# The first block's modulation rows: summed in column tiles of TensorE during the attentions and kept, in place of products on VectorE

## The chip, the cores and the metric

One core of one Trainium2 chip runs the whole program. The metric is the device time of one execution in microseconds. The kernel is written by hand for each engine's queue: PE (TensorE), ACT (ScalarE), DVE (VectorE), POOL (GpSimd) and SP (SyncE, which issues most weight loads). Everything is fp32.

## The reference

Two blocks of two layers each run on 256 latent tokens of width 1024 (two tiles of 128, called tiles 0 and 1). The second block also carries 256 context tokens (tiles 2 and 3).

```python
# first block, for l in 0, 1
mod = silu(c) @ w_ada[l] + b_ada[l]          # [1024] x [1024, 6144]
sh_m, sc_m, gt_m, sh_f, sc_f, gt_f = split(mod, 6)
h = rms_norm(x, g_pre_mix[l]) * (1 + sc_m) + sh_m
y = token_mixer(h, w_in[l], ..., w_out[l])   # two attentions, 8 heads each
x = x + gt_m * rms_norm(y, g_post_mix[l])
h = rms_norm(x, g_pre_ffn[l]) * (1 + sc_f) + sh_f
y = conv_glu_ffn(h, w_up_act[l], w_up_lin[l], ..., w_down[l])
x = x + gt_f * rms_norm(y, g_post_ffn[l])
# second block: an even layer (attention and short conv), then PEER experts,
# an odd layer (mLSTM), then PEER experts; rows for latents and for context
mod_l = split(silu(c_2) @ w_mod[i] + b_mod[i], 6); mod_c = the same with c_ctx_2
```

A modulation vector (6 of 1024 numbers a layer, 12 halves of 512) is one row, a product of one vector with a 25 MB matrix. What the kernel needs is the row spread over all 128 partitions, times a gain where there is one.

## The kernel before

**Streams and order.** The context's even layer, queries and first experts (`context`) don't depend on the first block, so each engine's program merges the two: `merged(first(lane, l), beside)` takes a step of the first block and then as many steps of the context stream as the shares (CH, ATT, PACE) ask for. All five queues are written in the same merged order, and every engine runs its queue in order. Four steps of the context stream (`AHEAD`) come before the first block begins. A background stream (`lane.run(mods, name)`) is taken a step at a time by `lane.fill(n, name)` and to its end by `lane.flush(name)`.

**Stages of the first block, each layer.** `lin` w_in (29 chunks of up to 512 KB), index scores, attention in ten steps of ATT 1.2 (layer 0) or 0.5 (layer 1), w_out in 8 chunks, feed-forward up in 44 chunks, down in 22. The context's queries (16 units, peer_w_q in two chunks every second unit) stand beside the attention of layer 0, and its 256 experts (each an indirect gather of 1 MB by POOL, a dot product on DVE L2244 and a weighted sum on PE L2186 or DVE L2239) beside all that follows.

**Modulation rows, three ways.** `Mods`: SP fetches pieces [128, 512] of the weight (256 KB), DVE multiplies each by a column of silu(c) and adds it to an accumulator (the first piece in L369, seven in L371), and PE sums over the partitions with a matmul of ones and adds the bias (L406, L408), which gives the row on all partitions; DVE (L381, L384) or ACT (L393) writes it into its place in MOD. `PairMods` (the context rows of layer 0 of the second block): no products; eight matmuls whose stationary operand is 32 columns wide, into four column groups of a bank by turns (L492), a bias matmul (L497), a copy on ACT (L516), a small DMA that keeps four rows in BR, and a matmul that adds and spreads the groups (L504). `KeptMods`: one matmul spreads a row kept in BR (L595). The first block uses `Mods` for all its halves, under these keys:

- ada0a (layer 0, shift and scale, 4 halves), at the start, after the four context steps, from 16 slots of 512 KB that were fetched early (`WIDE_L`);
- ada0b (layer 0, the other 8 halves), a quarter of a half behind each w_in chunk of layer 0, in 7 buffers of 256 KB;
- ada1a (layer 1, 6 halves), the same behind each feed-forward up chunk of layer 0;
- ada1b (layer 1, 6 halves), the same behind each w_in chunk of layer 1.

`keep1` and `keep2` are `Mods` too (w_mod of layer 1 of the second block, kept for later, 16 accumulators) and run in the context's even layer. The context's own rows come in `PairMods`: mod0c1 first of all, then mod0c2, a half behind each context step from the first on, through the four chunk buffers of RAW.

Of the kernel before, what the change touches and what calls it, by code (L numbers as in the profile page):

```python
# [118 lines left out]
def program(nc, D, out):  # L119
    with ExitStack() as ctx:  # L120
# [41 lines left out]
        def view(buf, a, *dims):  # L162
# [14 lines left out]
        AF = [T[:, 512 * i:512 * i + 512] for i in range(2)]  # L177
        OWN_T = [T[:, a:a + 512] for a in (1536, 3072, 3584)] + [HTt[:, 2048 + 512 * i:2560 + 512 * i] for i in range(4)]
        OWN_BIG = [BIG[:, 5632 + 512 * i:6144 + 512 * i] for i in range(3)] + [T[:, 1024 + 512 * i:1536 + 512 * i] for i in range(4)]
        ACS = [BIG[:, 512 * i:512 * i + 512] for i in range(2)]  # L180
# [5 lines left out]
        WIDE_L = [BIG[:, 1024 * i:1024 * i + 1024] for i in range(1, 7)] + [HTt[:, 1024 * i:1024 * i + 1024] for i in range(4)] + [  # L186
            T[:, 1024:2048]] + [SL[:, 1024 * i:1024 * i + 1024] for i in (3, 4, 8, 9, 10)]
        AHEAD = 4
# [84 lines left out]
        class Mods:  # L273

            def __init__(self, key, w, row0, jobs, accs, frees, guard=(), every=1, own=(), wide=()):
                self.own, self.named, self.wide = own, "own", wide
                self.ring = SIDE if not wide else FIRST[0] if accs else EARLY
# [155 lines left out]
        class PairMods(Mods):  # L434
# [3 lines left out]
            def __init__(self, key, w, row0, jobs, frees, guard=(), wide=()):  # L438
                Mods.__init__(self, key, w, row0, [(j, [(2, dst, kind, gain)]) for j, dst, kind, gain in jobs], None,
                              frees, guard, wide=wide)  # L440
                self.count = len(self.halves) + 1

# [39 lines left out]
            def sums(self, pe, q):  # L482
                j, hh, outs = self.halves[q]
                bk = bank(pe, self.ring, "pair", self.key, j, hh)
                pe.wait_ge(("silu",))
                for kh in range(4):
                    pe.wait_ge(("raw", self.key, j, hh, kh))
                    wt = self.pair_of(j, hh, kh)
                    for c in range(2):
# [3 lines left out]
                                            CP[:, 32 * kc:32 * kc + 32], wt[:, c, :],  # L493
# [16 lines left out]
            def copied(self, a, q):  # L510
                j, hh, outs = self.halves[q]
                a.wait_ge(a.last, ("mm", "pair", self.key, j, hh))
                if q >= 2:
                    a.wait_ge(("kept", *self.halves[q - 2][:2]), ("mm", "mod", self.key, *self.halves[q - 2][:2], 0))
                a.wait_ge(self.guard)
# [3 lines left out]
            def keep(self, a, q):  # L519
                j, hh, outs = self.halves[q]  # L520
                r = 48 + 4 * (2 * j + hh)
                a.wait_ge(("ev", "pair", self.key, j, hh))
                a.eng.dma_start(BR[r:r + 4, :], self.row(q)[0:128:32, :]).then_inc(*land.landed(f"kept{2 * j + hh}", "kept", j, hh))
# [5 lines left out]
            def dve(self, v):  # L529
                return self.each(v, lambda *_: None, self.out_dve)  # L530

# [28 lines left out]
        class KeptMods(Mods):  # L560
# [43 lines left out]
            def dve(self, v):  # L604
                return self.each(v, lambda *_: None, self.out_dve)

# [274 lines left out]
        def start_sp(sp):  # L881
# [4 lines left out]
            next(rows)  # L886
            sp.eng.dma_start(Xt[:, 2:4, :], D["ctx_2"].rearrange("(t p) d -> p t d", p=128)).then_inc(
# [3 lines left out]
        def second_rows_sp(sp):  # L891
            through(mods_of["start"].steps(sp))
# [2114 lines left out]
```

## Time and profile before

| | us |
|---|---|
| median of 3 runs | 3621.55 (3619.16 to 3630.48) |
| the profiled execution | 3621.2 |
| its span | 3619.9 |
| PE, DVE, ACT, POOL busy | 2892.3, 2313.7, 1136.4, 981.6 |
| DVE L371, products of the modulation rows, x280 | 212.7 |
| PE L492, PE L1114 | column tiles of the context rows; feed-forward up |

The page counts the fp32 matmuls in two records each, so x8 is four matmuls. Times in the rows are microseconds from the span's start unless ns is said.

### The profile page before, as it was taken

Reading aid. Unit: us, or ns where it says so; the run is one execution under the profiler, and the core shown is the slowest. Engines: PE = TensorE matmul, PEld = TensorE weight load, DVE = VectorE, ACT = ScalarE, POOL = GpSimd, SP = SyncE. Lnnn points to the kernel's source line nnn. Section 1 sums busy time; section 2 is a strip of 40 time slices with the busy share of each in tenths; the row PEclk is TensorE's granted clock in tenths of the full one; section 3 lists DMA queues with packets and bytes.
Section 4 is the critical chain, followed back from the end, with each engine's and each line's share of the span. In section 5 each row is a group of like instructions: output and inputs, shape, how many; then the busy total and the mean of one; then the engine's idle time right before and its main releaser. Section 6 shows DMA issues by size and latency. Waiting matters only on the chain.

```text
span 3619.9 us, 30466 instructions
## 1 busy us (share of the span) xinstructions
PE 2892.3 (80%) x9297; PEld 1538.4 (42%) x9297; DVE 2313.7 (64%) x4862; ACT 1136.4 (31%) x2905; POOL 981.6 (27%) x841
## 2 busy tenths in 40 slices
PE   5688967679988768987778777798779788777776
PEld 1344446356533336834446333343354463332222
DVE  0556538789867667875764998544423459975544
ACT  1112122323322352313451444333323224443333
POOL 0000000222332223332321444444310015443332
PEclk8789978689999889998879999899998889999999
DMA  8555732689979758997864999899962259999997
GB/s 333 173 191 204 248 123 94 227 343 363 358 288 409 273 205 323 417 408 262 315 242 157 392 421 421 347 420 421 421 238 75 70 211 419 421 421 421 422 421 332
DMA packets 214564, 1108.80 MB, mean 306 GB/s; under 512 B 24948, under 2 KB 25408, under 8 KB 116096
## 3 DMA queue, kind: packets, MB, share of 16 engines
q0 software_dynamic: 114512, 818.87, 56.1%
q1 hardware_dynamic: 99040, 287.27, 21.9%
q8 instruction: 73, 1.20, 0.1%
q10 hardware_dynamic: 848, 0.72, 0.1%
q14 instruction: 91, 0.75, 0.1%
HBM read 1105.58 MB, written 1.05 MB: 306 GB/s over the span
## 4 chain that ended last, share of the span: by engine, by line
PE 31%; DMA 29%; DVE 28%; ACT 4%; issue 4%; SPq 1%; POOL 1%; ACTq 0%; DVEq 0%; POOLq 0%
DMA AR<-in_uv,AR 24%; PE PS L805 9%; DVE AR L2244 7%; PE PS L2175 5%; PE PS L2088 3%; DMA AR<-in_w_in 2%; DVE AR L371 2%; PE PS L1127 2%; PE PS L1602 2%; DVE AR L2239 2%; PE PS L2186 2%; PE PS L787 1%; PE PS L2326 1%; DMA AR<-in_even_w_in 1%; DVE AR L1975 1%
## 5 line engine op out<-in xcount | busy, mean ns | idle before, releaser
L2294 POOL DMA_INDIRECT AR<-in_uv,AR x768 | 909.2, 1184 | 1577.9 <-PE PS L2175 641.3
L2244 DVE CUSTOM_DVE_ANT_0 AR<-AR 128x1024 f32<-128x1024 f32 x768 | 937.1, 1222 | 505.3 <-DMA AR<-in_uv,AR 503.2
L2175 PE MATMUL PS<-AR 128*128 128x512 f32 x2048 | 971.0, 622 | 288.6 <-ACT AR L2231 282.7
L2175 PEld LDWEIGHTS PS<-AR 128*128 128x128 f32 x2048 | 386.0, 196 | 867.1 <-ACT AR L2231 453.4
L805 PE MATMUL PS<-AR 128*128 128x512 f32 (+3 forms) x1080 | 470.5, 587 | 46.2 <-DMA AR<-in_w_in 20.8
L2213 ACT ACTIVATE AR<-AR 128x2 f32<-128x2 f32 x384 | 78.1, 203 | 1143.3 <-DVE AR L2244 1142.2
L1114 PE MATMUL PS<-AR 128*128 128x256 f32 x1408 | 322.1, 388 | 15.8 <-DMA AR<-in_w_up_lin 11.6
L805 PEld LDWEIGHTS PS<-AR 128*128 128x128 f32 x1080 | 204.1, 203 | 292.7 <-issue 241.7
L1114 PEld LDWEIGHTS PS<-AR 128*128 128x128 f32 x1408 | 269.9, 194 | 79.3 <-issue 19.7
L371 DVE SCALAR_TENSOR_TENSOR AR<-AR,CC 128x512 f32<-128x512 f32 x280 | 212.7, 760 | 67.5 <-DMA AR<-in_w_ada 44.6
L2231 ACT ACTIVATE AR<-C,AR 128x128 f32<-128x128 f32 (+1 forms) x614 | 241.0, 392 | 20.2
L2227 ACT ACTIVATE AR<-AR 128x1 f32<-128x1 f32 x768 | 226.1, 294 | 25.1
L2239 DVE SCALAR_TENSOR_TENSOR AR<-AR 128x1024 f32<-128x1024 f32 x152 | 196.4, 1292 | 9.2 <-ACT AR L2227 4.0
L2088 PE MATMUL PS<-AR 128*128 128x256 f32 x768 | 184.3, 402 | 4.0 <-DVE AR L641 3.2
L861 ACT ACTIVATE AR<-PS 128x256 f32<-128x256 f32 (+5 forms) x250 | 110.9, 443 | 234.5 <-PE PS L2088 113.3
L2213 ACT ACT_TABLE_LOAD x81 | 103.9, 1283 | 249.4 <-DVE AR L2244 249.3
L1127 PE MATMUL PS<-AR 128*128 128x512 f32 x352 | 161.6, 613 | 19.1 <-DVE AR L1357 8.3
L2186 PE MATMUL PS<-AR 64*64 64x512 f32 x816 | 126.8, 704 | 55.5 <-ACT AR L2231 53.8
L2088 PEld LDWEIGHTS PS<-AR 128*128 128x128 f32 x768 | 154.2, 204 | 28.0 <-issue 2.8
L1534 POOL TENSOR_TENSOR X<-X,AR 128x512 f32<-128x512 f32 x12 | 15.2, 1264 | 533.9 <-DVE AR L1526 533.9
L624 PE MATMUL PS<-C,AR 128*128 128x128 f32 x254 | 56.2, 393 | 117.4 <-DVE AR L714 47.8
L1127 PEld LDWEIGHTS PS<-AR 128*128 128x128 f32 x352 | 66.6, 195 | 113.6 <-issue 82.7
(235 smaller groups left out, 2652.4 us busy)
## 6 DMA issues: line engine op xcount, KB each, us to landing
AR<-in_w_ada SPq DMA_DIRECT2D x160, 256.0 KB, 8.1
AR<-in_w_in SPq DMA_DIRECT2D x56, 512.0 KB
AR<-in_w_mod SPq DMA_DIRECT2D x96, 256.0 KB, 4.5
AR<-in_peer_w_q SPq DMA_DIRECT2D x48, 512.0 KB
AR<-in_w_mod SPq DMA_DIRECT2D x45, 512.0 KB, 12.6
AR<-in_w_up_act SPq DMA_DIRECT2D x44, 512.0 KB
AR<-in_w_up_lin SPq DMA_DIRECT2D x44, 512.0 KB
AR<-in_w_down SPq DMA_DIRECT2D x44, 512.0 KB
```

The lines of the kernel that those rows point to most:

```text
L371: v.eng.scalar_tensor_tensor(out=acc, in0=wt, scalar=col, in1=acc, op0=ALU.mult, op1=ALU.add).then_inc(*v.done(*end))
L805: ins = pe.eng.matmul(bk[:, 0:n], lhs(k0 + kc, t), wt[:, kc, :], start=(k0 + kc == 0), stop=(k0 + kc == nk - 1))
L1114: ins = pe.eng.matmul(bk[:, f * 256:f * 256 + 256], wt[:, kc, cs], LAT.all[:, k0 + kc, :], start=(k0 + kc == 0 and f == 0), stop=(k0 + kc ...
L1127: ins = pe.eng.matmul(bs[t, hh], GT[:, f, t * 128:(t + 1) * 128], wt[:, 0, hh * 512:(hh + 1) * 512], start=(f == 0), stop=(f == 21))
L2088: ins = pe.eng.matmul(bk[:, f * 256:f * 256 + 256], wt[:, kc, cs], e.lay.all[:, k0 + kc, :], start=(k0 + kc == 0 and f == 0), stop=(k0 + k ...
L2175: ins = pe.eng.matmul(acc[i][hh], e.dg(x), e.buf(x)[:, 1024 + 512 * hh:1536 + 512 * hh], start=(x == e.on[False][i][0]), stop=(x == e.on[F ...
L2186: ins = pe.eng.matmul(acc[r][cols, :], e.dg(x)[rows, :], e.buf(x)[rows, 1024 + 512 * c:1536 + 512 * c], start=(x == e.on[False][x // 128][ ...
L2227: a.eng.activation(w, w, ACT.Copy, scale=gw_at(x // 16, x % 16, 1)).then_inc(*a.done(*(("w", e.key, x) if e.on_dve(x) else ())))
L2231: a.eng.activation(e.dg(x), cst("id2") if e.halved else ident, ACT.Copy, scale=w).then_inc(*a.done("dg", e.key, x))
L2239: v.eng.scalar_tensor_tensor(out=ACC, in0=row, scalar=w, in1=ACC, op0=ALU.mult, op1=ALU.add).then_inc(*v.done("sum", e.key, x))
L2244: v.eng.tensor_tensor_reduce(e.buf(x)[:, 0:1024], e.buf(x)[:, 0:1024], norm2(e).H[e.tiles[x // 128]], 1.0, 0.0, ALU.mult, ALU.add, DT[x // ...
L2294: g.eng.indirect_dma_start(e.buf(x), None, D["uv"][e.l], bass.IndirectOffsetOnAxis(ap=idx_at(x // 16, x % 16, 1), axis=0)).then_inc(*land. ...
```

## The change

The pieces of w_ada are no longer multiplied on DVE.

- **Start.** ada0a becomes `OneMods`, a `PairMods` with its own 32-wide columns `CP1` and without the DMA that keeps rows. Its steps run on every engine right behind mod0c1, ahead of the four context steps; those carry no mod0c2 half any more, since mod0c2 begins only after the fourth. The small conv rows are issued by POOL and no longer by SP; the context's norm is scaled early.
- **Layer 0, attention.** A stream "q", `Quads` "early", makes 12 halves: 8 of layer 0 and the 4 of layer 1's shift and scale. A step fetches four pieces [128, 512], one of each of four halves, and sums them with four matmuls of a 32-wide stationary operand, each half in its own column group of one bank. Eight steps and the biases make four halves; ACT copies the bank, and one DMA keeps four rows in BR (rows 112 to 127). There are five piece buffers (`OWN_Q`), in places of MOD and T, and SP waits for the score of the index (`("sco", 0, 1)`) before the first. One step stands before the attention, one behind each attention step, and one behind each of the context's query steps.
- **Layer 1, attention.** `Quads` "later" makes the other 8 halves of layer 1 the same way, with one step before, two behind each of the first five attention steps and one behind the others (`QUICK`).
- **Rows to their places.** `KeptAda` spreads a kept row with one matmul and lets DVE or ACT write it, as `KeptMods` does: 8 halves in each w_out (`fill(2)` a chunk), 4 halves in the feed-forward of layer 0. Nothing runs behind the w_in chunks.

```diff
+        OWN_Q = [MODt[:, 2048 + 512 * i:2560 + 512 * i] for i in range(3)] + [T[:, 3072 + 512 * i:3584 + 512 * i] for i in range(2)]
+        ROWS_Q = MODt[:, 3584:4096]
...
             def each(self, lane, made, put):
                 for q in range(len(self.halves)):
-                    if q:
+                    if q and not self.wide:
                         put(lane, q - 1)
                     made(lane, q)
+                    if q and self.wide:
+                        put(lane, q - 1)
                     yield
...
+        class Quads:
...
+            def sp(self, sp):
+                n = len(OWN_Q)
+                for q, (r0, halves) in enumerate(self.quads):
+                    for kc in range(8):
+                        for g, (l, r) in enumerate(halves):
+                            i = self.piece(q, kc, g)
+                            sp.wait_ge(("quad", self.key, i - n) if i >= n else self.guard)
+                            sp.eng.dma_start(OWN_Q[i % n], D["w_ada"][l][r, kc // 2, :, 512 * (kc % 2):512 * (kc % 2) + 512]).then_inc(
+                                *land.landed(f"quad{i % n}", "raw", self.key, i))
+                        yield
+                yield
+
+            def pe(self, pe):
+                n = len(OWN_Q)
+                for q, (r0, halves) in enumerate(self.quads):
+                    bk = bank(pe, SIDE, "quad", self.key, q)
+                    pe.wait_ge(("silu",))
+                    for kc in range(8):
+                        for g, (l, r) in enumerate(halves):
+                            i = self.piece(q, kc, g)
+                            pe.wait_ge(("raw", self.key, i))
+                            pe.eng.matmul(bk[32 * g:32 * g + 32, :], CC[:, kc:kc + 1].to_broadcast([128, 32]), OWN_Q[i % n],
+                                          start=(kc == 0), stop=False).then_inc(*pe.done("quad", self.key, i))
...
+                        yield
+                yield
+
+            def keep(self, a, q):
+                r0, halves = self.quads[q]
+                a.wait_ge(a.last, ("mm", "quad", self.key, q), ("kept", self.key, q - 1) if q else self.free)
+                a.eng.activation(ROWS_Q, psum("quad", self.key, q), ACT.Copy).then_inc(*a.done("ev", "quad", self.key, q))
+                a.wait_ge(a.last)
+                a.eng.dma_start(BR[r0:r0 + 4, :], ROWS_Q[0:128:32, :]).then_inc(*land.landed("keptq", "kept", self.key, q))
...
+        class KeptAda(KeptMods):
...
+            def spread_out(self, pe, q):
+                j, hh, outs = self.halves[q]
+                r = self.rows[j] + hh
+                bk = bank(pe, self.ring, "mod", self.key, j, hh, 0)
+                pe.wait_ge(self.made)
+                pe.eng.matmul(bk, ident[96:128, r:r + 1].to_broadcast([32, 128]), BR[96:128, :], start=True,
+                              stop=True).then_inc(*pe.done("mm", "mod", self.key, j, hh, 0))
...
+        def attended(lane, l, steps):
+
+            for i, _ in enumerate(steps):
+                lane.fill(1 + (i < QUICK[l]), "q")
+                yield ATT[l]
...
         def first_pe(pe, l):
             n1, n2 = norm_of["f", l, 1], norm_of["f", l, 2]
-            pe.run(mods_of["first", l])
-            for i, _ in enumerate(lin_pe(pe, ("win", l), D["w_in"][l], 8, (0, 3656), [0, 1], LAT.tile, prep=n1, ring=FIRST[l],
-                            whole=HEAD[l])):
-                if i >= 4 * len(HEAD[l]):
-                    pe.fill()
-                yield CH
-            pe.flush()
+            for _ in lin_pe(pe, ("win", l), D["w_in"][l], 8, (0, 3656), [0, 1], LAT.tile, prep=n1, ring=FIRST[l], whole=HEAD[l]):
+                yield CH
...
+            pe.flush("c")
+            pe.run(mods_of["quads", l], "q")
+            pe.fill(1, "q")
             yield 1.0
...
-            for _ in stages(8, s1, s2, s3):
-                yield ATT[l]
+            yield from attended(pe, l, stages(8, s1, s2, s3))
+            pe.flush("q")
+            pe.run(mods_of["first", l])
             yield 1.0
...
-                yield CH
+                pe.fill(2)
+                yield CH
+            pe.flush()
             pe.run(mods_of["next", l])
...
         def context(lane, even, queries, experts):
 
-            lane.run(cmods, "c")
             lane.run(Ready(keep1, keep2), "keep")
             for i, share in enumerate(even(lane, "c")):
+                if i == AHEAD - 1:
+                    lane.run(cmods, "c")
                 lane.fill(1 if i >= AHEAD else 0, "keep")
                 yield PACE * share
             lane.flush("keep")
             lane.run(cgate, "c")
             for share in queries(lane, of_ctx):
+                lane.fill(1, "q")
                 yield PACE * share
```

The other engines' programs of the first block are changed as `first_pe` is.

## Rows read from the trace of the kernel before

**Rows 1.** The page: chain by engine; GB/s in 40 slices.
```profile
PE 31%; DMA 29%; DVE 28%; ACT 4%; issue 4%; SPq 1%; POOL 1%; ACTq 0%; DVEq 0%; POOLq 0%
...
GB/s 333 173 191 204 248 123 94 227 343 363 358 288 409 273 205 323 417 408 262 315 242 157 392 421 421 347 420 421 421 238 75 70 211 419 421 421 421 422 421 332
```

**Rows 2.** Stretches: length, busy PE, PEld, DVE, ACT, POOL, clock, DMA share, GB/s.
```profile
0.00:50.00 50.00, 25.37 (x96) 7.28 (x96) 7.45 (x13) 10.86 (x19) 4.35 (x8) 0.81 0.98 377
134.00:460.00 326.00, 281.49 (x843) 145.45 (x842) 182.35 (x319) 50.16 (x119) 6.36 (x7) 0.92 0.67 228
541.00:627.00 86.00, 69.85 (x362) 59.92 (x361) 71.59 (x240) 24.28 (x84) 2.67 (x5) 0.86 0.27 89
740.00:960.00 220.00, 196.66 (x896) 143.61 (x895) 205.79 (x422) 74.19 (x151) 62.80 (x46) 0.97 0.98 379
1080.00:1240.00 160.00, 134.72 (x454) 57.85 (x452) 118.55 (x221) 38.23 (x95) 39.78 (x30) 0.95 0.92 365
1240.00:1345.00 105.00, 67.01 (x360) 39.66 (x360) 76.53 (x165) 51.75 (x139) 22.54 (x20) 0.76 0.53 187
```

**Rows 3.** Timeline of the start: us, duration, engine, line, operation.
```profile
46.24 0.36 SPq L253 DMA_DIRECT2D AR<-in_even_w_in  x1
...
59.39 5.88 PE L805 MATMUL PS<-AR 128*128 128x416 f32 x8 [14.60 <-DMA AR<-in_even_w_in]
...
93.67 0.49 DVE L369 TENSOR_SCALAR AR<-AR,CC 128x512 f32<-128x512 f32 x1
...
134.53 4.75 PE L805 MATMUL PS<-AR 128*128 128x512 f32 x8
```

**Rows 4.** Chain that ended last, in order of time, context steps.
```profile
76.86 3.03 DMA AR<-in_even_w_in
...
79.93 3.06 PE PS L805 x8
82.99 0.87 PE PS L504 x2
...
84.54 1.09 PE PS L492 x8
85.63 3.25 DMA AR<-in_even_w_in
```

**Rows 5.** Chain by line, 134 to 541 us.
```profile
by line: PE PS L805 30.7%; PE PS L1602 10.5%; PE PS L408 6.5%; DVE AR L371 5.8%; PE PS L406 5.7%; PE PS L2088 4.2%; DMA AR<-in_w_in 3.8%; DMA AR<-in_even_w_in 3.1%; issue 2.2%; PE PS L653 2.0%; DMA AR<-in_w_mod 1.8%; PE PS L492 1.7%; DVE AR
```

**Rows 6.** Line 302, SyncE's issues of 256 KB pieces: ns min/median/max, and landings.
```profile
L302 SPq DMA_DIRECT2D AR<-in_w_ada x160: 327/432/2986, 135.6 to 1191.6; - x160
...
DMA to landing us min/median/max: 2.5/5.0/23.7
```

**Rows 7.** Timeline, attention of layer 0: w_q chunk pairs (first, last of six), scores.
```profile
530.99 0.71 PE L2099 MATMUL PS<-AR 128*128 128x128 f32 x4
...
536.72 8.58 PE L2088 MATMUL PS<-AR 128*128 128x256 f32 x32 [0.87 <-ACT AR L861]
...
540.52 0.42 DVE L1414 TENSOR_TENSOR AR<-AR,C 128x256 f32<-128x256 f32 x1
...
616.57 7.13 PE L2088 MATMUL PS<-AR 128*128 128x256 f32 x32
```

**Rows 8.** Timeline, layer 1: the index scores are ready.
```profile
1245.30 0.42 DVE L1414 TENSOR_TENSOR AR<-AR,C 128x256 f32<-128x256 f32 x1
```

**Rows 9.** The page's DMA issues: a gain's broadcast.
```profile
MOD<-in_g_post_mix POOLq DMA_DIRECT2D x2, 512.0 KB, 7.0
```

**Rows 10.** DMA in 740 to 960 us, then in 1080 to 1240.
```profile
DMA packets 20157, 83.42 MB, mean 379 GB/s; under 512 B 2241, under 2 KB 2241, under 8 KB 14653
...
AR<-in_w_ada SPq DMA_DIRECT2D x46, 256.0 KB, 8.5
...
DMA packets 15320, 58.37 MB, mean 365 GB/s; under 512 B 1708, under 2 KB 1708, under 8 KB 11604
...
AR<-in_w_ada SPq DMA_DIRECT2D x44, 256.0 KB, 14.5
```

More of the change, by code:

```diff
@@ L886, in start_sp @@
             next(rows)
+            next(rows)
             sp.eng.dma_start(Xt[:, 2:4, :], D["ctx_2"].rearrange("(t p) d -> p t d", p=128)).then_inc(
@@ L916, in start_act, with second_rows_act @@
             first_rows(a)
+        def second_rows_act(a):
+            rows = mods_of["start"].steps(a)
+            next(rows)
+            next(rows)
+            next(rows)
+            norm_of["f", 0, 1].squares(a, ("pair", "ada0a", *mods_of["start"].halves[0][:2], 0))
+            through(rows)
         def start_dve(v):
@@ L1176, in first_pool @@
             n1, n2 = norm_of["f", l, 1], norm_of["f", l, 2]
[L1177 to L1180 removed]
+            for _ in lin(g, 8, (0, 3656), [0, 1], nothing, prep=n1):
                 yield CH
[L1182 removed]
             yield 1.0
@@ L1187, in first_pool @@
                     *land.landed(f"go{i}", "go", l, i))
+            g.flush("c")
+            g.run(mods_of["quads", l], "q")
+            g.fill(1, "q")
             yield 1.0
-            for _ in range(10):
-                yield ATT[l]
+            yield from attended(g, l, range(10))
+            g.flush("q")
+            g.run(mods_of["first", l])
             yield 1.0
             for _ in lin(g, 8, (0, 1024), [0, 1], nothing):
+                g.fill(2)
                 yield CH
+            g.flush()
             add_pool(g, l, 2, ("mix", l))
@@ L1298, in s2 @@
                                  ("mm", "av", l, u - 2) if u >= 2 else None).then_inc(*a.done("ev", "pt", l, u, kt))
-            for _ in stages(8, s1, s2, nothing):
-                yield ATT[l]
+            yield from attended(a, l, stages(8, s1, s2, nothing))
+            a.flush("q")
+            a.run(mods_of["first", l])
             for t in range(2):
@@ L1477, in s3 @@
                 v.events["ev", "av", l, u] = v.last
-            for _ in stages(8, s1, s2, s3):
-                yield ATT[l]
+            yield from attended(v, l, stages(8, s1, s2, s3))
+            v.flush("q")
+            v.run(mods_of["first", l])
             rs = []
@@ L1494, in first_dve @@
             for _ in lin(v, 8, (0, 1024), [0, 1], nothing):
+                v.fill(2)
                 yield CH
-            add_dve(v, l, 2, ("lin", "wout", l), mods_of["first", 0] if l == 0 else mods_of["next", 0])
+            v.flush()
+            add_dve(v, l, 2, ("lin", "wout", l), mods_of["first", l])
             v.run(mods_of["next", l])
```

208 lines of the change are left out of this document (128 added, 80 removed).

## The prediction

> **What bounds the kernel now.** I read the page first. No engine is full over the span, and the chain that ended last is shared by PE, DMA and VectorE [rows 1]: a change is worth what it does to the stage it lies in, so everything below goes by stage. The changed work all lies in the front, before 1400 us; behind it the slices are at 420 GB/s of gathered experts, which the change doesn't touch, so what the front gains or loses should come out at the end.
>
> The table by stretches [rows 2] cuts the front at its stages. To 134 us (the start) the first 50 us are a full DMA, then it falls away. From 134 to 460 PE is busy over 80% (projections of both streams). From 541 to 627, and again from 1240 to 1345, lie the attentions of the first block: DMA moves only 89 and 187 GB/s. From 740 to 960 (feed-forward of layer 0) and from 1080 to 1240 (projection of layer 1) DMA runs at 379 and 365 GB/s, and in the first VectorE is busy 206 of 220 us as well.
>
> **The start.** The timeline [rows 3] and the chain [rows 4] show it. SyncE issues w_ada, x and small conv rows up to 46.2 us, and only then the first even_w_in chunk, which PE uses at 59.4. Each of the four context steps that follow takes 8.8 us (76.86 to 85.63), of which 3.06 are its matmuls; the rest is one half of the context rows. At 93 VectorE begins the 32 products of ada0a, some 26 us of work, and PE begins w_in only at 134.5. After the change the conv rows leave SyncE's queue, the four steps carry no half, and the four halves of ada0a are summed on PE as they land. By bytes: 377 GB/s over 50 us [rows 2] is 18.9 MB, just the 16.8 MB of these weights and the two inputs, so all are in at about 50, the last row made about 3.5 us later, 56 at most. Four context chunks and two turns on PE are some 18 us (53 to 72), then conv rows 1.3, norm and turn of the latents about 7: w_in starts at 80 instead of 134.5. **-54** (bounds -45, -60).
>
> **134 to 541.** Three context halves were made here; now all seven steps of that stream are. A step costs 5.7 us beyond its chunk where nothing else runs [rows 4], and also uses up the four chunk buffers; I take 7 each, +28 for four (bounds 15, 35). Gone are the 8 halves of ada0b. The chain's shares of VectorE's products (L371) and of the two matmuls a half (L406, L408) are 5.8, 5.7 and 6.5%, 18% of these 407 us [rows 5], 73 us for 24 accumulators (8 of ada0b, 16 of the keeping streams). A third is 24; with VectorE and SyncE also less in the way of the others I take 30 (bounds 24, 45). Together **-2**.
>
> **The attentions.** This is where the change pays. 96 pieces of 256 KB, 24 steps of four, go into the attention of layer 0, and 64 in 16 steps into that of layer 1. In layer 0 a step is put behind each attention step and behind each query step of the context, about three to an attention step, so they are through after some seven; nothing is left to flush. Column tiles four at a time: before, eight records (four matmuls) take 1.09 us, one full 512-column matmul 0.87 [rows 4], so I take 1.1 us of PE for a step. The price is the wait. There are five buffers, and SyncE may issue piece i only when PE has used i-5; its issue takes 0.43 us, and a piece of these queues needs 2.5 us at the least and 5.0 in the middle [rows 6]. The third of a step's four issues is what the next step needs: 3 times 0.43 plus 2.5 to 5.0 is 3.8 to 6.3, so a step can't follow the last in under about 5 us. SyncE's queue has the w_q chunks behind these waits, one step ahead only. In layer 0 two w_q chunks come each 16 us (536.72 to 616.57, five gaps) [rows 7], of which 7 us are the chunk's matmuls; with it 7+1, then two steps at 5, one of them covered by attention's own work, is 18: +2.1 us, 7.5 times, +16. Besides, the first piece waits for the scores, ready at 540.9 [rows 7], while PE stands at its first step since some 531 and has the score matmuls of unit 0 and w_q behind it; with some 4.5 us to land and a second step before unit 0, VectorE gets it at some 552 instead of 541: +11. Layer 0: **+27** (bounds 10, 55). In layer 1 five attention steps of 8 us carry two steps each: 5 of PE's own work, 1, then 5 of waiting is 11, five times +3; six single ones at +1; the scores are ready at 1245.7 [rows 8], +6. That is **+27** (bounds 12, 55).
>
> The Trainium skill, in DMA: Bandwidth & Descriptors, section Anatomy of one DMA, puts a transfer at 2.0 us plus its bytes by 436 GB/s; the estimate for a step by it (2.0 us and four pieces) is 4.4 us, and the sum would be some 14 us lower. The loaded landings of [rows 6] are slower than it, so I stay at 5. Its TensorEngine Tiling (Array Packing), section Key Properties, speaks against the change: switching the tiling mode drains the engine, and here 40 steps switch it to and fro. The 1.09 us of [rows 4] came right behind full-width work, so a drain of 0.2 us, 8 us over 40 steps, is already in my 1.1; a larger one no row shows.
>
> **The output projections.** Eight halves of kept rows are spread in each (0.87 us of PE, +7), and now right where the gains arrive: POOL issues each gain with its half, a broadcast takes 7.0 us to land [rows 9], VectorE waits for it, and PE's next half waits for the one bank. Three gains, some 4 us beyond a chunk's 3.6 each, would be 12; gathers are waited for there anyhow, so I take 5. **+12** in each layer (bounds 7, 20).
>
> **Feed-forward of layer 0.** Out go 46 of ada1a's 48 pieces that were issued here, 12 of 83.42 MB [rows 10]: 71.4 MB at 379 GB/s are 188 us against 220. VectorE loses 42 products and 6 first ones, 34.5 of 205.8 us, to 171; PE loses 12 matmuls, 12.9 us, and gets 4, 3.5 us, 187 left of 196.7 [rows 2, 10]. DMA and PE meet at 188: **-30** (bounds -18, -34).
>
> **Projection of layer 1.** 44 pieces, 11.5 of 58.37 MB, which at about 400 GB/s are 29 us; nearly all the stretch is at that rate, and PE's 134.7 us go to 123 [rows 2, 10]. With the pieces just ahead of it, **-30** (bounds -20, -34).
>
> **Sum.** -54 -2 +27 +12 -30 -30 +27 +12 = -38. The profiled execution took 3621.2 us (span 3619.9); the median of the runs is 3621.55, so the two are one. I predict **3583 us**.
>
> **Rivals.** (1) Slower: the five-piece ring is the new bottleneck of both attentions. A step costs two waits a round in layer 0 (15 us of span for each us of the step's time) and about 7 us for each us in layer 1. From 5 to 8 us (w_ada pieces took 8.5 where DMA was full [rows 10]) that is +66: 3649. It decides from about 6.7 us a step on. For it: in-order PE, and SyncE behind the same waits; against: DMA has room there. (2) No change: the freed bytes of the two full stretches come to nothing, because PE, already busy 197 of 220 and 135 of 160 us, sets them. Then they give 10 each, and the sum is +2: 3623. (3) The start's gain goes back, the seven context steps now standing in a stretch where PE is 85% busy with 8.8 us each and the relief of VectorE there off the path: +7 and +15 on the second term, 3605. (4) Better: waits in the attentions are covered by VectorE, busy 72 of 86 us there [rows 2], and cost half, 27 in all for both; the projections 7 each: 3546.
>
> **How the numbers follow.** A measurement of this kernel tells 0.3%, 11 us, from nothing. My forecast, with (3) as its weaker form, 0.52; (4) 0.15; (2) 0.12; (1) 0.21. Faster is the forecast's and (4)'s 0.67, same 0.13, slower 0.20. The forecast's own range is 3555 to 3608; for 8 in 10 it reaches toward (1) and past (4): 3532 to 3636.
>
> **What would show it.** First w_in matmul near 80 us; in both attentions PE waiting for in_w_ada, steps 5 us apart, the stretches 541 to 627 and 1240 to 1345 each some 27 us longer; no L371 on w_ada, 112 left for keeping; the feed-forward stretch at some 190 us with VectorE under 90%; the projection of layer 1 at 130. The prediction is wrong if a step in the attentions takes over 6.7 us, if w_in starts later than 95, or if the feed-forward stays above 205.

## The result and the profile after

| | before | after |
|---|---|---|
| median of 20 runs each | 3622.41 (3612.43 to 3632.04) | 3638.92 (3626.26 to 3649.85) |
| ratio | | 1.0042, interval 1.0033 to 1.0052 |
| profiled execution | 3621.2, span 3619.9 | 3629.07, span 3627.8 |

The changed kernel is 0.42% slower, 16.5 us by the medians. The forecast was 3583 us, faster, with a range to 3636: the sign was wrong, and the median lies 3 us above the range. The profiled execution is one of the faster ones, so its trace shows 8 of the 16.5 us; the runs spread over 24 us, and where the other 8 lie no trace here shows.

The page after, its chain by engine, which answers to [rows 1], and two rows of its groups:

```profile
PE 41%; DMA 29%; DVE 19%; ACT 5%; issue 3%; POOL 2%; SPq 1%; ACTq 0%; DVEq 0%; POOLq 0%
...
L665 PE MATMUL PS<-MOD,CC 128*32 128x512 f32 x194 | 83.7, 693 | 59.6 <-DMA MOD<-in_w_ada 50.0
L370 DVE SCALAR_TENSOR_TENSOR AR<-AR,CC 128x512 f32<-128x512 f32 x112 | 86.4, 772 | 44.5 <-DMA AR<-in_w_mod 40.6
```

The products are gone from VectorE as foreseen (112 of 280 left, 28% of the chain down to 19), but PE's share went from 31 to 41%. The windows of the attention of layer 0, the feed-forward up of layer 0, the attention and the w_out zone of layer 1, which answer to [rows 2] (same columns):

```profile
472.00:648.00 176.00, 142.70 (x644) 74.22 (x645) 91.76 (x300) 32.42 (x109) 8.62 (x11) 0.91 0.68 235
752.00:938.00 186.00, 182.27 (x881) 137.47 (x881) 170.89 (x378) 74.21 (x151) 62.89 (x45) 1.00 0.97 371
1187.00:1291.00 104.00, 74.13 (x416) 28.87 (x416) 54.39 (x131) 40.83 (x111) 13.14 (x14) 0.83 0.82 278
1291.00:1392.00 101.00, 64.01 (x200) 25.89 (x196) 41.02 (x61) 25.25 (x62) 20.53 (x17) 0.79 0.55 195
```

The feed-forward stretch is 186 us at 371 GB/s, VectorE 170.9 busy, as forecast. The attention of layer 0 is 176 us, with VectorE busy only 92 of them.

The next table cuts both traces, and those of four experiments below, at the same places: first 512-column w_in matmul, second score of the index ready (VectorE), last value matmul of the attention, first up matmul, last down matmul, and so on for layer 1. The place "last value matmul" is the start of the value matmuls of the last two of the eight units in layer 0 and of the last unit in layer 1. Each entry is a stretch's length less that of the kernel before, in us, from the starts of matmuls and instructions in the traces (before: 134.5, 406.0, 106.1, 92.3, 304.0, 202.4, 65.2, 71.8, 247.1).

```
                    forecast  after  a_start  d_ring9  g_all  m_late_T
start                  -54    -50.1   -50.3    -50.4   -50.0   -50.5
to scores, layer 0      -2    -18.8   +29.5    -19.1   -19.0   -17.5
attention 0            +27    +69.9    +0.1    +31.9   +24.3   +21.7
w_out zone 0           +12    +11.9    -1.4    +12.0    +4.8    +2.9
feed-forward 0         -30    -37.3    -0.1    -34.5   -29.9   -29.8
to scores, layer 1     -30    -33.8    +1.4    -33.1   -35.3   -35.2
attention 1            +27    +38.7    -0.4    +25.6   +21.3   +17.5
w_out zone 1           +12    +29.4    +0.2    +24.9   +15.2   +13.6
feed-forward 1           0     -1.4    -1.4     -1.6    +1.9    +3.7
sum, last down         -38     +8.5   -22.3    -44.2   -66.6   -73.6
```

The two attentions and the w_out zone of layer 1 took 72 us more than their terms. Three other terms gave 28 more than forecast, and the start 4 less. Inside the attention of layer 0, PE's timeline, with the first w_in matmul ahead (the last column is the idle time before a row and who ended it):

```profile
84.46 4.31 PE L905 MATMUL PS<-AR 128*128 128x512 f32 x8
...
474.69 3.56 PE L665 MATMUL PS<-MOD,CC 128*32 128x512 f32 x4 [12.18 <-DMA MOD<-in_w_ada]
...
484.32 0.72 PE L1177 MATMUL PS<-AR 64*128 64x128 f32 x8
...
490.22 7.14 PE L2211 MATMUL PS<-AR 128*128 128x256 f32 x32 [0.30 <-DMA AR<-in_peer_w_q]
...
501.91 1.04 PE L665 MATMUL PS<-MOD,CC 128*32 128x512 f32 x2 [1.49 <-DMA MOD<-in_w_ada]
...
505.14 0.71 PE L1177 MATMUL PS<-AR 64*128 64x128 f32 x8
```

PE stands 12 us at the first piece; the score matmuls of unit 0 (L1177) start 12.7 us after the scores of the index, where before they came 5.4 us ahead of them. Unit 1 follows 21 us later, against 14 before. VectorE takes unit 0 13 us after it has finished the scores, where the kernel before did it at once:

```profile
485.18 0.89 DVE L1568 SCALAR_TENSOR_TENSOR AR<-PS,C 128x256 f32<-128x256 f32 x2 [13.15 <-PE PS L1177]
```

SyncE's wait for the scores, before it may issue the first piece, is called the guard below. The waits of 484 to 648 us (who waited for whom: us, times, longest):

```profile
ACT AR L1405 <- DVE SM L1575: 68.9, 7, 18.6
DVE AR L1568 <- PE PS L1177: 61.6, 8, 13.1
...
PEld PS L665 <- DMA MOD<-in_w_ada: 29.0, 20, 3.0
PEld PS L665 <- DMA AR<-in_w_ada: 18.1, 13, 2.7
```

All eight units of VectorE wait for the scores on PE, 61.6 us, and PE in its turn waits for pieces. SyncE's issues of pieces in that window (ns; first and last start):

```profile
L651 SPq DMA_DIRECT2D MOD<-in_w_ada x58: 327/430/646, 472.1 to 631.8; - x58
L651 SPq DMA_DIRECT2D AR<-in_w_ada x38: 327/428/1984, 473.4 to 627.8; - x38
```

96 pieces from 472.1 to 631.8 us are 24 steps, 23 intervals, 6.9 us apart in the mean. The forecast had 5, and put the point from which the other sign decides at 6.7. The mean spacing holds everything else that PE does in the stage, too; what it can tell is taken up below.

In the w_out zone of layer 1 VectorE shows one reason, and PE what it waits for:

```profile
1354.82 0.08 DVE L2367 DVE_READ_ACCUMULATOR2_ANT AR<- 128x1 f32 x1
1363.24 0.69 DVE L380 TENSOR_TENSOR MOD<-PS,MOD 128x512 f32<-128x512 f32 x1 [8.33 <-PE PS L704]
1371.36 0.69 DVE L380 TENSOR_TENSOR MOD<-PS,MOD 128x512 f32<-128x512 f32 x1 [7.43 <-PE PS L704]
...
1373.43 1.54 DVE L1360 SCALAR_TENSOR_TENSOR AR<-PS,SM,MOD 128x512 f32<-128x512 f32 x2
```

```profile
1354.33 7.76 PE L887 MATMUL PS<-AR 128*128 128x512 f32 x16
1362.02 1.12 PE L704 MATMUL PS<-BR,C 32*128 32x512 f32 x2
```

L380 writes the two halves of g_post_ffn's row. Nothing reads them before the end of the feed-forward, but they stand in front of the sums (L1360) that the norm waits for, and each waits for a spreading matmul (L704) behind 7 us of w_out matmuls that were held back to the end (L887).

### The profile page after: what moved, and what is told of

It is laid out like the page before. It is cut to its first block, busy times and chain, and to the rows that moved or that the text cites. A ratio compares the mean times of both kernels' runs of the same rounds, so it can differ in the third digit from the quotient of the medians.

```text
span 3627.8 us, 30891 instructions
## 1 busy us (share of the span) xinstructions
PE 2939.8 (81%) x9681; PEld 1516.2 (42%) x9681; DVE 2177.4 (60%) x4671; ACT 1141.5 (31%) x2914; POOL 972.2 (27%) x853
## 3 DMA queue, kind: packets, MB, share of 16 engines
HBM read 1105.58 MB, written 1.05 MB: 305 GB/s over the span
## 4 chain that ended last, share of the span: by engine, by line
PE 41%; DMA 29%; DVE 19%; ACT 5%; issue 3%; POOL 2%; SPq 1%; ACTq 0%; DVEq 0%; POOLq 0%
DMA AR<-in_uv,AR 23%; PE PS L905 10%; DVE AR L2367 6%; PE PS L1232 5%; PE PS L2298 5%; PE PS L2211 4%; PE PS L2309 2%; PE PS L1725 2%; DMA AR<-in_w_ada 2%; PE PS L1245 2%; PE PS L887 1%; PE PS L665 1%; POOL AR L2417 1%; PE PS L2449 1%; DMA MOD<-in_w_ada 1%
## 5 line engine op out<-in xcount | busy, mean ns | idle before, releaser
L2417 POOL DMA_INDIRECT AR<-in_uv,AR x768 | 893.7, 1164 | 1611.0 <-PE PS L2298 658.0
L2298 PEld LDWEIGHTS PS<-AR 128*128 128x128 f32 x2048 | 387.7, 197 | 865.2 <-ACT AR L2354 449.5
L905 PE MATMUL PS<-AR 128*128 128x512 f32 (+3 forms) x1080 | 453.2, 571 | 16.0 <-ACT AR L961 6.0
L1232 PE MATMUL PS<-AR 128*128 128x256 f32 x1408 | 317.0, 384 | 2.0 <-DVE AR L741 1.1
L905 PEld LDWEIGHTS PS<-AR 128*128 128x128 f32 x1080 | 198.4, 198 | 250.8 <-issue 225.4
L1232 PEld LDWEIGHTS PS<-AR 128*128 128x128 f32 x1408 | 265.5, 191 | 64.5 <-issue 18.4
L2211 PE MATMUL PS<-AR 128*128 128x256 f32 x768 | 179.1, 393 | 6.8 <-DVE AR L741 3.2
L2211 PEld LDWEIGHTS PS<-AR 128*128 128x128 f32 x768 | 150.2, 198 | 35.1 <-issue 7.5
L665 PE MATMUL PS<-MOD,CC 128*32 128x512 f32 x194 | 83.7, 693 | 59.6 <-DMA MOD<-in_w_ada 50.0
L370 DVE SCALAR_TENSOR_TENSOR AR<-AR,CC 128x512 f32<-128x512 f32 x112 | 86.4, 772 | 44.5 <-DMA AR<-in_w_mod 40.6
```

The lines of the kernel that those rows point to most:

```text
L905: ins = pe.eng.matmul(bk[:, 0:n], lhs(k0 + kc, t), wt[:, kc, :], start=(k0 + kc == 0), stop=(k0 + kc == nk - 1))
L1232: ins = pe.eng.matmul(bk[:, f * 256:f * 256 + 256], wt[:, kc, cs], LAT.all[:, k0 + kc, :], start=(k0 + kc == 0 and f == 0), stop=(k0 + kc ...
L2211: ins = pe.eng.matmul(bk[:, f * 256:f * 256 + 256], wt[:, kc, cs], e.lay.all[:, k0 + kc, :], start=(k0 + kc == 0 and f == 0), stop=(k0 + k ...
L2298: ins = pe.eng.matmul(acc[i][hh], e.dg(x), e.buf(x)[:, 1024 + 512 * hh:1536 + 512 * hh], start=(x == e.on[False][i][0]), stop=(x == e.on[F ...
L2417: g.eng.indirect_dma_start(e.buf(x), None, D["uv"][e.l], bass.IndirectOffsetOnAxis(ap=idx_at(x // 16, x % 16, 1), axis=0)).then_inc(*land. ...
```

## The experiments

Times are medians; each ratio is to the kernel before on the same chip.

**a_start**: one part alone. The new start stays, `Quads` and `KeptAda` go, `Mods` make ada0b, ada1a and ada1b as before.

```diff
-mods_of["first", 0] = KeptAda("ada0b", 0, {2: 112, 4: 114, 3: 116, 5: 118}, ...)
+mods_of["first", 0] = ada("ada0b", 0, (2, 4, 3, 5), AF, {0: n1r, 1: n1r}, n1t, OWN_T)
...
```

> One part alone: the new start (column-tile rows for the first norm, the new order of the wide loads, convolution rows on POOL's queue, the context's rows begun one step later), with every other modulation row made on VectorE as in the kernel before. Theory 1 (the start's gain is real and stays; what turned the change into a loss is the attentions, where TensorE's queue stands at the pieces of the weights): 3565 to 3605 us, first w_in matmul at 84 us instead of 134.5, attentions as long as before (106 and 65 us from the scores to the last value product). Theory 4 (the gain of the start is given back further on, whatever the attentions do): 3615 to 3625 us.

3614.01 us (3599.05 to 3628.83), ratio 0.9974, 0.9961 to 0.9987. This lies in neither range: w_in starts at 84, but of the 50 us the stretch to the scores takes 29.5 back (table), by the four context halves that moved there, and the rest stays: 22 in the profile, 10 in the median. The attentions are as before. So the loss of the whole change isn't in the start. The kernel after is 48 us shorter than this one up to the scores, which is what the eight halves of ada0b cost there. Chains by line, first of a_start from 84 to 520, then of the kernel after from 84 to 472:

```profile
by line: PE PS L908 26.3%; PE PS L1724 11.6%; PE PS L410 6.0%; DMA AR<-in_even_w_in 5.9%; DVE AR L373 5.8%; PE PS L408 5.5%; PE PS L2210 3.8%; DMA AR<-in_w_in 3.5%; DMA AR<-in_w_mod 2.7%; PE PS L499 2.5%; issue 2.2%; PE PS L511 1.7%; PE PS 
```

```profile
by line: PE PS L905 35.2%; PE PS L1725 11.8%; PE PS L407 4.3%; PE PS L2211 4.2%; PE PS L405 4.0%; DMA AR<-in_w_mod 3.9%; DMA AR<-in_w_in 3.5%; DMA AR<-in_even_w_in 2.6%; PE PS L753 2.3%; PE PS L496 2.3%; DVE AR L370 2.2%; issue 2.0%; PE PS 
```

The products and the two matmuls a half are 17.3% of 436 us, 75, in the one, and 10.5% of 388 us, 41, in the other: 34 of the 48 us.

**b_nofetch**: no transfers and no waits for pieces but the first five of each run.

```diff
-sp.wait_ge(("quad", self.key, i - n) if i >= n else self.guard)
-sp.eng.dma_start(OWN_Q[i % n], ...)
+sp.wait_ge(None if i >= n else self.guard)
+if i < n:
+    sp.eng.dma_start(OWN_Q[i % n], ...)
...
-pe.wait_ge(("raw", self.key, i))
+pe.wait_ge(("raw", self.key, i % n))
```

> The changed kernel in which only the first five pieces of each of the two runs of pieces are fetched; the matmuls of the other pieces read the five buffers as they stand, so the rows of the first block are not the reference's, and 39 MB are not moved. It takes the waits for pieces and their bytes away and leaves TensorE the same matmuls. Theory 1 (waits at the ring of five buffers): the attention of layer 0 falls from 176 us to 120 to 135, that of layer 1 from 104 to 75 to 85, the total 3560 to 3590 us. Theory 2 (the time of the column-tile matmuls on TensorE, 58 and 42 us busy, is what is paid): the attentions stay above 160 and 95 us and the total above 3615 us.

3565.15 us, ratio 0.9843, 0.9826 to 0.9859. Attentions 132.8 and 79.6 us. Every number lies in the ranges of theory 1. The run takes away the waits and the bytes together; d_ring9 below keeps the bytes. The same two waits as above, 474 to 606 us:

```profile
ACT AR L1406 <- DVE SM L1576: 36.4, 7, 7.1
DVE AR L1569 <- PE PS L1178: 21.2, 4, 11.9
```

VectorE's wait falls from 61.6 to 21.2. The attention of layer 0 gets 43 us shorter and that of layer 1 24. What is left, 27 us above before in layer 0, is as much as the forecast charged with all waits.

**c_narrow**: waits kept, PE's time taken out.

```diff
+w = 512 if kc == 0 else 16
-pe.eng.matmul(bk[32 * g:32 * g + 32, :], ..., OWN_Q[i % n],
+pe.eng.matmul(bk[32 * g:32 * g + 32, 0:w], ..., OWN_Q[i % n][:, 0:w],
```

> The changed kernel in which the matmuls of seven of the eight row chunks of each piece run cover 16 columns instead of 512: all transfers and all waits stay, most of TensorE's time for them is left out, and the rows are not the reference's in the columns left out. Theory 1 (waits): little changes, 3615 to 3640 us, the attention of layer 0 still above 150 us. Theory 2 (TensorE's time): 60 us or more come back, 3580 us or below, attention of layer 0 below 130 us.

3638.74 us, ratio 1.0041, 1.0027 to 1.0056; attentions 180.3 and 110.2. Theory 2 falls: under the waits PE's time for the pieces is worth nothing that shows (the clock fell with it, see the last section).

**d_ring9** and **h_ring7**: nine and seven buffers.

```diff
-OWN_Q = [MODt[:, 2048 + 512 * i:2560 + 512 * i] for i in range(3)] + [T[...] for i in range(2)]
+OWN_Q = [MODt[:, 512 * i:512 * i + 512] for i in range(7)] + [T[...] for i in range(2)]
```

The guard and the frees of rows 0 and 1 get the norm's readers and the quads' sums besides; h_ring7 takes MODt from column 1024 on.

> The changed kernel with nine buffers for the pieces instead of five (rows 0 and 1 of the modulation area are idle between the first norm and w_out), the same guard on the scores. Theory 1 (a ring too short for the time of a transfer): steps of an attention 15 to 18 us apart instead of 21, the attention of layer 0 130 to 150 us, the total 3595 to 3620 us. Rival 1a (not the depth of the ring but the rate of the transfers in this stretch): steps still 20 us or more apart and 3630 to 3645 us. Theory 2 (TensorE's time): 3632 to 3642 us.

> Seven buffers, guard as in the changed kernel. Theory 1 (the ring's depth sets the pace): halfway between five and nine, attention of layer 0 150 to 162 us and the total 3598 to 3615 us. Rival 1a (seven already cover a transfer): attention of layer 0 138 to 145 us and 3575 to 3590 us.

d_ring9: 3576.78 us, ratio 0.9877, 0.9858 to 0.9896; h_ring7: 3602.60, ratio 0.9940, 0.9921 to 0.9959. Five, seven, nine buffers give 3639, 3603 and 3577 us, and an attention of layer 0 of 176, 157 and 138 us: there the depth sets the pace, with the same bytes moved. In layer 1 it is not so even: 104, 103 and 91 us, so two more buffers gave nothing there and the next two all of the 13 us. Seven met their range (their trace is of the slowest of four runs), nine gave 18 us more than the edge of theirs. SyncE's issues in the attention of layer 0 with nine, then the same waits:

```profile
L651 SPq DMA_DIRECT2D MOD<-in_w_ada x76: 327/432/1658, 471.5 to 593.2; - x76
```

```profile
ACT AR L1405 <- DVE SM L1575: 35.2, 7, 7.1
...
DVE AR L1568 <- PE PS L1177: 25.5, 5, 13.1
```

Steps are 5.3 us apart now, and VectorE's wait is 25.5 (34.3 with seven), close to the 21.2 without any wait but for the first pieces. In layer 1 the windows suggest what stops nine buffers from giving more:

```profile
1152.00:1243.00 91.00, 72.56 (x416) 30.09 (x416) 54.54 (x131) 40.84 (x111) 14.70 (x14) 0.84 0.94 343
```

The DMA engines are busy 0.94 of it at 343 GB/s, against 0.82 and 278 after. So two steps behind each unit probably meet the rate of the transfers there and no longer the ring; no run separates the two.

**i_ring9_narrow** and **k_nofetch_narrow**: the narrow matmuls again, once the waits are less (nine buffers) or gone.

> Nine buffers with the guard of the changed kernel, and the matmuls of seven of the eight row chunks over 16 columns instead of 512 (the rows are not the reference's in the columns left out). With five buffers the narrow matmuls changed nothing, because the waits took their place. If with nine buffers TensorE's own time for the pieces is what is left above the 106 us of before (theory 2 as what stands behind theory 1), the attention of layer 0 falls from 138 to 115 to 127 us and the total from 3577 to 3545 to 3562 us. If the rate of the transfers is still what is left: attention of layer 0 133 to 140 us and 3568 to 3585 us.

> Only the first five pieces of each run fetched, and the matmuls of seven of eight row chunks over 16 columns: neither the waits for pieces nor most of TensorE's time for them (the rows are not the reference's). It tells what the 27 us are by which the attention of layer 0 without transfers is still longer than before (133 against 106 us). If they are TensorE's busy time for the pieces, in order ahead of the scores and w_q: attention of layer 0 106 to 118 us, of layer 1 66 to 74 us, total 3535 to 3553 us. If they are not (what is left is the clock that falls with narrow matmuls, or the order of the queues): attention of layer 0 125 us or more and 3558 us or more.

3582.88 us (ratio 0.9889, 0.9869 to 0.9910; attentions 138.9 and 92.2) and 3551.98 us (0.9810, 0.9784 to 0.9837; 125.2 and 74.6). With nine buffers the narrow matmuls give nothing. Without transfers they give 13 us in all, 7.6 in the attention of layer 0 and 5.0 in that of layer 1. In layer 0 I had expected 15 to 27 if PE's time were the whole: the total lies in that range, the attention at the edge of the other. So PE's time for the pieces is some part of the last 27 us there, and 19 us stay without it. The places show more, in us: scores to first score matmul, from there to that of the last unit, from there to the last value matmul.

```
before              -5.4   96.8  14.7
after               12.7  150.6  12.7
b_nofetch           11.4  106.0  15.4
k_nofetch_narrow    11.0   99.4  14.8
d_ring9             12.6  113.0  12.4
e_ring9_early        4.9  114.3   9.3
g_all                5.1  116.3   9.1
m_late_T            -4.4  122.8   9.4
```

In b and k the score matmuls of unit 0 come 17 us later than before (first column), behind the first piece, which waits for the scores. About 5 of these were slack: VectorE takes unit 0 12 and 11 us after the scores, against at once before. That is 12 of the 27 us in b and 11 of the 19 in k.

**e_ring9_early**: seven of the nine buffers don't wait for the scores.

```diff
-sp.wait_ge(("quad", self.key, i - n) if i >= n else self.guard)
+sp.wait_ge(("quad", self.key, i - n) if i >= n else self.guard if i == 7 else self.first if i == 0 else None)
```

> Nine buffers, and the seven of them that lie in the modulation area are filled as soon as the first norm has read it, before the scores are ready; only the two in T still wait for the scores. Theory 1 with its second part (TensorE stood 12 us at the first piece because all pieces wait for the scores): the first score matmul of the attention comes about 10 us after the scores are ready in neither layer, and the total falls by 10 to 22 us from the 3577 us of the nine buffers alone, to 3555 to 3567 us. Rival (that wait only stood in the place of another, the first pieces run beside other transfers): 3570 to 3582 us.

3570.83 us (3557.80 to 3579.53), ratio 0.9846, 0.9824 to 0.9869. That is inside the rival's range, and d_ring9's interval overlaps, so the gain is not told from nothing by the runs. In its trace the two attentions are 9.6 and 3.5 us shorter than d_ring9's, and the stretch to the scores, where seven pieces are now fetched, is 4 us longer. PE's timeline tells what is left of the wait:

```profile
478.40 1.92 PE L665 MATMUL PS<-AR,CC 128*32 128x512 f32 x2 [9.59 <-DMA AR<-in_w_ada]
480.24 1.01 PE L1177 MATMUL PS<-AR 64*128 64x128 f32 x6
```

Piece 7 lies in T (AR), so it still waits for the scores, and it belongs to the second step, which stands ahead of unit 0.

**m_late_T**: as g_all (below), with the two buffers in T used for the first time by the twelfth and thirteenth piece (numbers 11 and 12, counted from 0).

```diff
+at = list(range(7)) + [0, 1, 2, 3, 7, 8, 4, 5, 6] * 11
-... OWN_Q[i % n] ...
+... OWN_Q[at[i]] ...
```

> As g_all, but the two buffers in T are used for the first time by pieces 11 and 12, behind the score matmuls of unit 0 in TensorE's queue. In g_all piece 7 lies in T, so it waits for the scores and TensorE stands 10 us at it with the score matmuls of unit 0 behind it. If this wait is what remains of the guard: the first score matmul comes before the scores are ready and not 5 us after, the attention of layer 0 goes from 134 to 120 to 127 us, of layer 1 from 87 to 78 to 86 us, and the total is 3532 to 3547 us. If VectorE's own queue sets the start of the attention: the first score matmul earlier, but the attention and the total within 5 us of g_all (3550 to 3560 us).

3552.09 us, ratio 0.9794, 0.9777 to 0.9812, beside g_all's 0.9813: the rival's range. Its attentions are 127.8 and 82.7 us, g_all's 130.5 and 86.5, and the first score matmul does come before the scores, as the theory wanted. PE and then VectorE in m_late_T:

```profile
463.34 1.06 PE L667 MATMUL PS<-MOD,CC 128*32 128x512 f32 x8
...
468.11 0.72 PE L1179 MATMUL PS<-AR 64*128 64x128 f32 x8
...
475.61 1.59 PE L667 MATMUL PS<-AR,CC 128*32 128x512 f32 x2 [4.52 <-DMA AR<-in_w_ada]
479.71 8.67 PE L2213 MATMUL PS<-AR 128*128 128x256 f32 x32 [2.51 <-DMA AR<-in_peer_w_q]
```

```profile
472.98 0.88 DVE L1570 SCALAR_TENSOR_TENSOR AR<-PS,C 128x256 f32<-128x256 f32 x2
...
492.24 0.88 DVE L1570 SCALAR_TENSOR_TENSOR AR<-PS,C 128x256 f32<-128x256 f32 x2 [10.10 <-PE PS L1179]
```

Unit 0 is now on time: VectorE takes it the moment that the scores are ready, as before the change. But the guard only moved: the T piece of the third step waits 4.5 us and the w_q chunk behind it 2.5, and VectorE waits 10.1 us for unit 1 instead. In the places above, 9.5 us left g_all's first column and 6.5 came back in the second.

**f_last**: five buffers, the halves of g_post_ffn made in the feed-forward.

```diff
-mods_of["first", 0] = KeptAda("ada0b", 0, {2: 112, 4: 114, 3: 116, 5: 118}, ...)
+mods_of["first", 0] = KeptAda("ada0b", 0, {2: 112, 4: 114, 3: 116}, ...)
+mods_of["last", l] = KeptAda(f"ada{l}c", l, {5: 114 if l else 118}, {3: quads.kept()}, quads.kept())
...
-lane.run(mods_of["next", l])
+lane.run(Ready(mods_of["last", l], mods_of["next", l]))
```

> The changed kernel (five buffers) with the two halves of g_post_ffn's row, which nothing reads before the end of the feed-forward, made in the feed-forward and not in w_out. Theory 3 (these halves stand in VectorE's queue ahead of the sums that w_out's norm waits for): w_out zone of layer 0 from 104 to about 96 us and of layer 1 from 101 to 80 to 88 us, the total 3612 to 3628 us. Rival (the sums wait for w_out's own matmuls, the rows are beside them): zones unchanged and 3633 to 3643 us.

3621.65 us, ratio 0.9999, 0.9987 to 1.0011. Theory 3 holds in size: 17 us of the medians, the zones 94.8 and 91.0 instead of 104.2 and 101.2. Layer 0's gave 9 of its 12 us, as expected; that of layer 1 only 10 of 29, short of the 80 to 88 us expected.

**g_all**: nine buffers, early pieces and late halves together.

> Nine buffers, early pieces and the last halves in the feed-forward together. If the three costs lie at three places and add up: 3577 less 10 to 22 less 15 to 27, so 3530 to 3552 us, 2% or more faster than the kernel before. If they cover for each other: 3555 to 3575 us.

3555.29 us (3550.91 to 3563.04), ratio 0.9813, 0.9794 to 0.9831. That is 21.5 us less than d_ring9, by the late halves and early pieces. It lies at the edge of the covered case and above the sum of all three, but it beats both kernels: 69 us below before, 84 below after. Of the versions that compute every row m_late_T has the lowest median; its interval overlaps that of g_all.

**j_poolq**: g_all with the pieces issued by POOL.

```diff
-return {"pe": self.pe, "sp": self.sp, ...}
+return {"pe": self.pe, "pool": self.sp, ...}
```

> The version of g_all with the pieces issued from POOL's queue instead of SP's, so that the w_q chunks no longer stand behind pieces that wait for a buffer. If what is left in the attention of layer 0 is that order in SP's queue (the chain of waits has 15 us of w_q chunks): attention of layer 0 from 134 to 120 to 128 us, the total 3535 to 3550 us. If w_q is paced by its own ring: 3550 to 3560 us. If the gathers of the experts on POOL's queue now stand behind the pieces: 3565 us or more.

3569.00 us, ratio 0.9854, 0.9838 to 0.9871; attentions 134.0 and 96.5, for 130.5 and 86.5 in g_all. The w_q chunks behind pieces in SyncE's queue are not what is left of layer 0, and layer 1 got 10 us longer. Its 64 pieces now stand in the queue that issues the gathers, and each issue takes 536 ns there (430 on SyncE); that this is the cause is likely and was not tested.

## Why the prediction was wrong, by its steps

**What bounds the kernel, and the start.** Right: 84 us for 80, -50 for -54. That some of it goes back through the moved context halves was in the sum at +28; a_start measured 29.5. Why the median of a_start keeps only 10 of the 22 us that its trace keeps is open.

**134 to 541.** The +28 was right, the -30 for ada0b too small: a_start against after gives 48, a little past its bound of 45. Of this 34 are products and matmuls of the chain, where a third of [rows 5] had been 24; the rest is how the other work closes up.

**The attentions: the step that failed.** It is the price of the waits for pieces: 2.1 us a round, 7.5 times, +16 in layer 0, and five times 3 and six times 1, +21, in layer 1. b_nofetch, without these waits and bytes, gave back 43 us in layer 0 and 24 in layer 1. With all the bytes, nine buffers gave back 38 and 13.

Under it lay "a step can't follow the last in under about 5 us", with one such wait a step and one of two covered. The landing of a piece was right; h_ring7 in 470 to 640 us, for 2.5/5.0/23.7 in [rows 6]:

```profile
DMA to landing us min/median/max: 2.7/5.5/16.4
```

What was wrong is what the ring has ready when PE comes back. It holds the next step and one piece, and SyncE issues piece i when PE has used i-5. While PE does something else (7 to 8 us of w_q), nothing new is issued for it. After a w_q chunk one step finds its pieces, and the next starts and waits inside: in the kernel after, steps start at 497.7, 499.4, 506.4, 518.3 and 520.0 us. From its first matmul to its last, the 24 steps of layer 0 take 87 us of PE's time after, 49 in d_ring9 and 34 in b_nofetch. And PE is in order: the scores stand behind, and VectorE waited for them (61.6 us).

The mean spacing of steps is a poor measure of this. By their first matmuls it is 7.2 us after and 5.5 in d_ring9, but still 5.4 in b_nofetch, where all but the first pieces are there. So the sign "over 6.7 us" came true, but the spacing also holds all other work. Rival 1, with its 15 us for each us of a step, gives 56 at 6.9 for a measured 70. It had the mechanism and the sign, and a chance of 0.21; that its size is near is in part luck, since it took the spacing for the cause.

The prediction worked out 4.4 us a step by the Trainium skill, DMA: Bandwidth & Descriptors, section Anatomy of one DMA, and stayed at 5. The fit there is for transfers issued from GpSimd, and these pieces are SyncE's. By it one piece would land in an estimated 2.6 us: that is near the least that h_ring7 shows (2.7), and half of the median (5.5).

The guard's +11 was about right: VectorE takes unit 0 13 us after the scores in layer 0, against at once before. In layer 1 it is 13.7 against 2.3, +11 for the +6 of the forecast. PE's own time was right: a step that finds its pieces takes 1.06 us, for the 1.1 assumed, even directly between full-width matmuls (L2224), here in m_late_T:

```profile
505.17 0.61 PE L2224 MATMUL PS<-AR 128*128 128x128 f32 x4
505.71 1.06 PE L667 MATMUL PS<-MOD,CC 128*32 128x512 f32 x8
506.70 0.71 PE L2224 MATMUL PS<-AR 128*128 128x128 f32 x4
```

The Trainium skill's TensorEngine Tiling (Array Packing), section Key Properties, says that a switch of tiling mode drains the engine. The ends of matmuls are modelled in a trace, but the starts are 0.99 us apart here, so these rows show no drain beyond what the 1.09 us of [rows 4] already had.

Of the sum itself two small things: a round of 18 us against 15.97 is +2.0 and not +2.1, and the windows taken for the attentions (541 to 627, 1240 to 1345) are not the attentions, which by the places run from 541 to 647 and from 1245 to 1311.

**The output projections.** Layer 0's +12 came true by luck: the term was 7 us of PE and 5 for landings of gains, but f_last shows that 9 of the 12 were the last halves' place in VectorE's queue. In layer 1 it was 29 for 12: the term left out that the last halves wait there for PE's held matmuls, ahead of the sums. Moving them took 10 off. 14 to 19 us remain in the versions with late halves (25 in those without). Some 4 us of this are spreading matmuls in the chain (L704, four of 1.05 us each in g_all); the rest is not settled.

**Feed-forward 0 and projection 1.** Right in mechanism: -37 and -34 for -30 and -30; DVE 170.9 for 171, 371 GB/s for 379. The granted clock was 1.00 there against 0.97 [rows 2], for which nothing had been charged.

**Rivals 2, 3 and 4.** The freed bytes did pay (2 falls), the second stretch gave 19 us where rival 3 had it cost 20 (3 falls), VectorE covered nothing (4 falls: it was the one that waited).

**Open.** What the last 22 us of the attention of layer 0 are in the best version (m_late_T). The guard's wait moves on when it is taken away, and transfers and PE's time each explain only a part. One wait stands in every version and was not tried: all sums of four halves go through one bank, so the first matmul of the next four waits until ACT has copied it, and ACT has the softmax's exponentials in front. In m_late_T:

```profile
516.96 1.94 PE L667 MATMUL PS<-MOD,CC 128*32 128x512 f32 x8 [5.07 <-ACT MOD L681]
```

PE waits 6.2 us so in the attention of layer 0, in two waits, and 5.6 in that of layer 1 (after: 6.2 and 3.9). What a second bank would give no run shows. Finer interleaving (two pieces between the parts of a unit) wasn't tried either. Nor is it settled why the medians of after and a_start lie 10 to 15 us above their profiled executions and those of d_ring9 and g_all only up to 3.

## What to carry to other kernels

Work put into the idle time of an in-order queue brings the waits for its slowest input with it, and everything behind it in the queue waits too. Price the wait at every turn of the ring, not once, and count how many buffers cover a landing plus the time that the engine is away. When a stream of small transfers is moved to a stretch with free bandwidth, look for buffers that are idle there; here four more were worth 62 us by the medians (52 by the traces), more than the whole change had cost. And place in a queue what is needed late behind what is needed now.

## What the runs showed of the hardware

Where the pieces' matmuls covered 16 columns instead of 512, the granted clock of the stretch was lower and their neighbours were slower. In the attention of layer 0 the clock was 0.91 after and 0.72 in c_narrow, 0.93 in d_ring9 and 0.82 in i_ring9_narrow, 0.87 in b_nofetch and 0.81 in k_nofetch_narrow. The w_q matmuls in 472 to 600 us, of the kernel after and of c_narrow:

```profile
L2211 PE MATMUL PS<-AR 128*128 128x256 f32 x164 | 38.9, 397 | 3.6 <-DMA AR<-in_peer_w_q 3.0 <-ACT AR L961 0.7
```

```profile
L2212 PE MATMUL PS<-AR 128*128 128x256 f32 x160 | 47.2, 466 | 2.9 <-DMA AR<-in_peer_w_q 1.8 <-ACT AR L1406 1.1
...
L666 PE MATMUL PS<-MOD,CC 128*32 128x16 f32 x68 | 5.7, 205 | 12.3 <-DMA MOD<-in_w_ada 12.3
```

